# A Trainium2 transformer kernel: in 64 half panels the matrix products of 512 and 256 columns are grouped instead of alternated, and the group of 512 waits for less

## The reference

```python
hn = rmsnorm(h, norm_mix[l])
proj = jnp.einsum('bsd,de->bse', hn, w_in[l])          # first block: gq, gk, gv are columns of it
qkv = jax.nn.silu(causal_dwconv(jnp.concatenate([gq, gk, gv], axis=-1), gdn_conv_w[l]))
...
h2 = rms_norm(x, norm2_g[l])                            # second block, 2816 columns each
x = x + (jax.nn.silu(h2 @ w_gate[l]) * (h2 @ w_up[l])) @ w_down[l]
```

## Time and profile before

| | |
|---|---|
| median of 3 runs | 804.54 us (804.46 to 804.77) |
| the profiled execution's own time | 805.96 us |
| its span, first to last instruction | 804.6 us |
| PE busy | 797.8 us (99%) |
| PE weight loads busy | 699.9 us (87%) |
| DVE busy | 596.8 us (74%) |
| ACT busy | 448.1 us (56%) |
| chain that ended last | PE 97%, of it L584 94% |
| products of 512 columns in "hl" | 512 of them, of 256 columns as many |

### The profile page before, as it was taken

One profiled execution on the slowest core, in us unless ns is written; L12 is line 12 of the kernel. 1 busy time (PEld: TensorE's weight loads), 2 busy tenths in 40 slices (PEclk: granted clock), 3 DMA queues, 4 the chain that ended last, 5 costly groups with the idle time before them and its releaser, 6 DMA issues.

```text
span 804.6 us, 13127 instructions
## 1 busy us (share of the span) xinstructions
PE 797.8 (99%) x5176; PEld 699.9 (87%) x5176; DVE 596.8 (74%) x1009; ACT 448.1 (56%) x727; POOL 75.0 (9%) x65
## 2 busy tenths in 40 slices
PE   8999999999999999999999999999999999999998
PEld 6888888999898888899999998887878888888886
DVE  6898989785555766679999996486766777778543
ACT  6577677554535544456656564366665655655431
POOL 0001000000011302101101110021100111011000
PEclk9999999999999999999999999999999999999999
DMA  9645564557442555475687665555425656656641
GB/s 316 185 158 158 166 231 147 161 145 227 122 119 89 171 173 203 162 241 177 199 247 243 216 202 196 175 186 175 142 82 170 203 176 205 196 172 208 194 151 74
DMA packets 118062, 144.09 MB, mean 179 GB/s; under 512 B 11489, under 2 KB 86641, under 8 KB 117745
## 3 DMA queue, kind: packets, MB, share of 16 engines
q1 hardware_dynamic: 115552, 141.22, 54.6%
q10 hardware_dynamic: 2448, 2.03, 1.1%
HBM read 141.78 MB, written 1.46 MB: 178 GB/s over the span
## 4 chain that ended last, share of the span: by engine, by line
PE 97%; DVE 1%; DMA 1%; ACT 0%; issue 0%; SPq 0%; DVEq 0%; ACTq 0%
PE bank L584 94%; PE bank L638 1%; DMA panel_raw<-in_w_in 1%; DVE conv_acc L1631 1%; PE bank L960 0%; PE bank L682 0%; PE bank L909 0%; DVE panel_lo L1595 0%; PE bank L933 0%; PE bank L660 0%; PE bank L737 0%; PE bank L839 0%; SPq L2400 0%; ACT panel_hi L1106 0%; DVE h L2024 0%
## 5 line engine op out<-in xcount | busy, mean ns | idle before, releaser
L1595 DVE TENSOR_TENSOR panel_lo<-panel_raw,panel_hi 128x1024 fp32r<-128x1024 f32 x245 | 308.0, 1259 | 138.9 <-ACT panel_hi L1106 138.5
L584 PE MATMUL bank<-x_halves,panel_hi 128*128 128x256 f32 (+1 forms) x1536 | 368.3, 322 | 0.7 <-DVE x_halves L2031 0.7
L1106 ACT ACTIVATE panel_hi<-panel_raw 128x1024 fp32r<-128x1024 f32 (+1 forms) x247 | 260.4, 1055 | 176.6 <-PE bank L584 174.6
L584 PE MATMUL bank<-x_halves,panel_lo 128*128 128x256 f32 x1024 | 289.1, 282 | 0.0
L584 PEld LDWEIGHTS bank<-x_halves,panel_hi 128*128 128x128 f32 x1536 | 257.0, 191 | 23.3 <-issue 0.9
L584 PEld LDWEIGHTS bank<-x_halves,panel_lo 128*128 128x128 f32 x1024 | 195.7, 191 | 0.2
L584 PE MATMUL bank<-panel_hi,x_halves 128*128 128x512 f32 x384 | 122.0, 399 | 0.0
L584 PEld LDWEIGHTS bank<-panel_hi,x_halves 128*128 128x128 f32 x384 | 70.0, 188 | 14.4 <-DVE panel_lo L1595 0.6
L584 PE MATMUL bank<-panel_lo,x_halves 128*128 128x512 f32 x192 | 75.1, 391 | 0.0
L584 PE MATMUL bank<-panel_hi,act_hi 128*128 128x512 f32 x176 | 68.6, 390 | 0.0
L584 PE MATMUL bank<-panel_hi,act_lo 128*128 128x512 f32 x176 | 68.5, 389 | 0.0
(11 more groups left out here) (291 smaller groups left out, 913.1 us busy)
## 6 DMA issues: line engine op xcount, KB each, us to landing
panel_raw<-in_w_in SPq DMA_DIRECT2D x35, 1024.0 KB, 5.3
panel_raw<-in_w_up SPq DMA_DIRECT2D x30, 1024.0 KB, 5.2
panel_raw<-in_w_down SPq DMA_DIRECT2D x20, 1024.0 KB, 5.0
panel_raw<-in_w_gate SPq DMA_DIRECT2D x10, 1024.0 KB, 5.3
panel_raw<-in_w_out SPq DMA_DIRECT2D x8, 1024.0 KB, 5.1
panel_raw<-in_w_in SPq DMA_DIRECT2D x11, 512.0 KB, 5.5
panel_raw<-in_w_branch_fox SPq DMA_DIRECT2D x4, 1024.0 KB, 5.0
panel_raw<-in_w_branch_gdn SPq DMA_DIRECT2D x4, 1024.0 KB, 5.1
```

The source lines that it names most:

```text
L584: return e.matmul(o, l, r, start=start, stop=stop, skip_group_check=True)
L1106: return e.activation(o, i_, ACT.Copy, scale=scale)
L1595: e.tensor_tensor(lo, raw_view(i, k0, kt), hi.bitcast(F32), ALU.subtract).then_inc(s_lo, 1)
```

## The change

In "hl" the two products of a row tile no longer alternate. For each j all four products of 512 columns come first, in the order of k, and then the four of 256 columns. The wait for the half panel is split too: the first product now waits for the high part alone (`s_hi`), and the wait for the low part (`s_lo`) stands ahead of the first product with `panel_lo`. Number, size and operands of the products, their banks and the signals to other engines stay as they were.

```diff
                     if j == 0:
-                        e.wait_ge(*landed)
+                        e.wait_ge(*((s_hi, n) if how == "hl" else landed))
...
                         if how == "hl":
                             mm(o, hi[:, k, js], HALVES_OF[x][:, :, kx, :], begin and k == 0, False)
-                            i_ = mm(o[:, 0:T], lo[:, k, js], xh[:, kx, :], False, last and k == kt - 1)
                             continue
...
+
+                    if how == "hl":
+                        if j == 0:
+                            e.wait_ge(s_lo, n)
+                        for k in ks:
+                            i_ = mm(o[:, 0:T], lo[:, k, js], xh[:, kp + k0 + k, :], False, last and k == kt - 1)
```

## The result

The changed kernel takes 805.54 us (median of 21 runs, 805.38 to 807.0), the kernel before 804.53 us (21 runs, 804.21 to 806.5): ratio 1.0012, 95% interval 1.0006 to 1.0017. It is slower by 1.0 us, clear of noise but under the 0.2% (1.6 us) that I had set as the bound. The profiled execution has a span of 804.3 us, shorter than the 804.6 of before. That is no contradiction: what stands ahead of n = 5 took 1.35 us less in it (the first "hl" product starts at 23.37 us, and at 24.72 in the profile before). The difference is TensorE's clock in n = 1. In the profile before, the mean granted clock from 10.78 to 16.00 us is 0.67, and from 11.28 to 13.84 us every three products of 256 columns take 0.64 us; in the profile after the clock is 1.00 there and three such products take 0.36.

A forecast was written before the change was run, and what follows sets the result against it. PE's stream of matrix products was taken to bound the kernel, at the 2.4 GHz level throughout. Waits 0, octets +2.05 us and conv stage alternation -0.99 us sum to +1.06 us on 804.54, giving 805.6 us, range 803.1 to 808.3.

The forecast's parts named there:

- The relaxed wait: Half panel start: beginning on the high part alone gains 0 us, since in up2 the low part is 5.7 us early.
- the added wait: One more wait in mid-run in each of 64 half panels: taken as 0 us, bound 5.1 us.
- Rival 4: Mid-run wait breaks the stream, weight loads not fetched across it: +4.1 us, 808.7; chance 0.12 together with other small costs.
- The unsettled alternation of the conv stage: Some 148 alternating pairs take 353.3 ns, not 346.7; the new order removes this, -0.99 us.
- The doubt that DVE would take part of it: Conv stage: part of the gain lies before the DVE stretch at 34 to 38 us, where a faster PE only waits.
- +16 ns per octet: Each of 128 grouped octets loses 23 ns entering the 512s and regains 7 ns: +2.05 us in all.
- The sum, +1.06 us: Whole kernel: +2.05 us for the octets and -0.99 us for the conv stage's alternation, giving 805.6 us.
- The reason that I gave: In the octets: products of 512 lose time after the run of 256 before them, until they settle.
- The row that I took (+23, -7): Earlier trace: four 512s after a settled run of 256 lose 23 ns; going from 512 to 256 regains 7 ns.
- Rival 2: Both stages: order is neutral, every octet at its floor, 803.55 us or 804.5; chance 0.20.
- Rival 3: Each octet loses the full 40 ns, +5.12 - 0.99 = +4.1 us, 808.7, mainly in up2; chance 0.20.
- Rival 5: Faster by over 1.6 us: -7 ns at each octet without loss plus the conv stage's gain, 802.6; chance 0.10.

The follow-up runs named there:

- experiment 2: Kernel before, alternating order kept, with only the split wait of the change: 804.53 us against 804.49, ratio 1.0.
- experiment 1: Kernel before with the grouped order of the change but the old wait, none in mid-run: 805.42 us against 804.49, ratio 1.0012.
- experiment 4: Kernel before with grouping in the conv stage's 20 half panels alone, alternating in up2, split wait in both: 804.13 us against 804.49, ratio 0.9996.
- first sweep: Experiment 5: kernel before, old wait, a different order or alternation for each pair of up2's panels: 806.0 us in one execution, against 804.42.
- experiment 8: Kernel before with groups of two (hhllhhll) in all 64 half panels, old wait: 804.49 us, ratio 1.0003.
- experiment 3: Kernel before with grouping in up2's 44 half panels alone, alternating in the conv stage, split wait in both: 805.87 us against 804.49, ratio 1.0018.
- experiment 9: Kernel before with groups of two in one single half panel, n = 191, alternation in all others: 806.86 us against 804.50, ratio 1.0033.
- experiment 7: Kernel before with groups of two (hhllhhll) in the conv stage, alternation in up2, old wait: 804.13 us against 804.50, ratio 0.9997.

## Why the prediction was right, step by step

**The relaxed wait, 0 us, and the added wait, 0 us.** Shown by experiment 2, with up2 at 123.17 us as before. Rival 4 falls with it, and experiment 1 says the same from the other side.

**The unsettled alternation of the conv stage, -0.99 us.** The term counts 148 pairs, of which 140 are in the conv stage (-0.93 us) and 8 in n = 187. The new octets' 40 x 16 ns come on top: -0.29 us for the stage by my own terms. Measured -0.32 in the profile after and -0.36 between the medians of experiment 4. That the parts agree so well is partly luck. The doubt that DVE would take part of it was right in kind: PE's wait for `kT` grew by 0.1 us, and n = 9 takes 3.70 us instead of 3.66. At n = 31, where the second octet waits for its bank, more is lost (2.95 us instead of 2.87). Against that stand gains beyond the 0.02 us a half panel that my terms give: 0.08 us in n = 15, and 0.04 us each in the "wide" half panels n = 7 and 13, which stand behind an "hl" one and had no term (2.75 us instead of 2.78).

**+16 ns per octet.** In up2 it is 16.7 (33.3 ns a half panel). The distances within an octet are the ones read from the earlier trace rows: in the profile after, where "down" is entered, they show as they did there, and in up2 the run of four takes the same 0.93 us. The distances between products of 512 don't fall evenly towards 0.227, though, as the prediction had it: one octet of up2 has 233, 236, 228, 232 ns and the next 235, 233, 236, 224.

```profile
741.56 0.40 PE L584 MATMUL bank<-panel_hi,act_hi 128*128 128x512 f32 x1
...
742.49 0.39 PE L584 MATMUL bank<-panel_hi,act_lo 128*128 128x512 f32 x1
```

**The sum, +1.06 us; measured +1.01.** 805.6 was forecast against the runs' median and 805.54 came. The agreement within 0.1 us is better than the argument deserved, as the next point says.

**What was wrong in it.** The reason that I gave, that the loss is paid each time 512 follows 256, and is longer the less a run can settle, is not how it works in general. The row that I took (+23, -7) holds for four and four, and for eight and eight too: in the first sweep the eight of 512 take 1.84 us (657.96 to 659.80) where eight at the settled pace take 1.81, and with the return that is the measured +20 ns. It fails for shorter groups. Groups of two pay less with twice the changes (experiments 5 and 8), and alternation pays nothing or 53 ns a half panel with the same eight changes. The steady pace belongs to the whole repeated order, and for alternation even to how it was entered. Had each change cost 16 ns, groups of two would have come out 3 us slower, and they cost nothing. Rival 2, that the order is neutral, falls in both stages: the new octets take 2.807 us a half panel in up2 and, undisturbed, in the conv stage too (n = 6), not 2.773. Rival 3, that the full 40 ns of the earlier trace rows are paid, falls by the 16.7 measured. Rival 5 falls by the interval.

**The clock.** The granted clock was not at its top throughout: a slice of the earlier trace rows is 20 us long, and its digit hides the few microseconds at the lower level in n = 1. No distance that the sum uses lies there, so the forecast doesn't suffer by it.

The rule of N / 2.4 + 2.5 ns from the Trainium skill (TensorE: Matmul & The Clock Gate, Back-to-back issue gap), given there for a single product's gap, has no term for the order. Experiments 1, 3 and 9 don't agree with it: the granted clock was 1.0 in their profiled executions, and the same products of up2 took 1.38, 1.38 and 2.10 us more in another order.

**What stays open.** What the state is that the stream carries from one product to the next, and why a half panel's excess comes in near multiples of 6.7 ns (13, 20, 33, 53), that is 16 cycles of the 2.4 GHz clock. No experiment here touched the reads of weights and moving columns, or the banks, apart from their order. The order is shown to be the cause of the time, and what in the engine makes it so is not. No version was clearly faster than the kernel before: experiments 4 and 7 are 0.4 us under it by their medians, within their intervals.

## What to carry to other kernels

In a stream of products with no idle time, compare starts, not busy time: the distance between neighbours over a whole repeated unit shows a loss of 2% (2.83 us against 2.77) that no wait and no busy share shows. Look at the granted clock in narrow windows and not only in the page's slices before comparing two spans. Where products of different sizes take turns, as here, measure the price of each order for itself, and expect that a settled alternation can be put into a dear form by a few products ahead of it, or by a break; check the pace at both ends of a stage before and after any edit near it. A relaxed wait is worth only what it was late: read from the trace how far ahead the other engine is, before splitting one.

## What the runs showed of the hardware

- Pace of fp32r products of 128 x 128 weights at the full granted clock: 226.7 ns for 512 columns and 120.0 for 256, so 13.3 ns over the columns' time at 2.4 GHz, in runs of one size. At the 1.2 GHz level in n = 1 of the profile before, three of 256 columns take 0.64 us where three take 0.36 at the full clock.
- Alternating, a pair takes 346.7 or 353.3 ns, and keeps the one it has: over 39 half panels in experiment 9. The dear form repeats every three pairs (232, 118, 241, 120, 236, 113 ns between starts), the cheap one is 230, 117, or 231, 113, 233, 117. The same instructions went on in either form behind a break (n = 32: 2.77 us before, 2.83 in experiment 9).
- A wait that is already met, at the start of a run or in the middle of one, cost nothing that 11 runs could tell (804.53 against 804.49 us for 64 of them), nor the traces (up2 123.17 us with and without 44 of them).
